# The delta rule's block inverse: VectorE's block transpose for the second orientation of levels 1 to 5

## Chip, cores and metric

The kernel runs on one core of a Trainium2 chip, as one launch. The metric is the device time of the launch in microseconds; the trace gives the span of the core, which is about 2 us shorter.

## What is computed

Two transformer blocks on 256 tokens of width 1024 in fp32: a gated delta rule with a short convolution, sparse attention, MLPs, spatial gating, stick-breaking attention. The change lies in the first mixer, the delta rule. For each of 8 heads and each chunk of 64 tokens the reference solves with a unit lower triangular matrix:

```python
m_low = jnp.where(strict, jnp.einsum('nbhik,nbhjk->nbhij', kb, kc) * decay, 0.0)
a_mat = m_low + jnp.eye(c, dtype=f32)
u = lax.linalg.triangular_solve(a_mat, vc * bc[..., None], left_side=True, lower=True, unit_diagonal=True)
w = lax.linalg.triangular_solve(a_mat, kb * jnp.exp(gc)[..., None], left_side=True, lower=True, unit_diagonal=True)
attn = jnp.einsum('nbhik,nbhjk->nbhij', qc, kc) * decay
...
v_new = u_c - jnp.einsum('bhck,bhkv->bhcv', w_c, state)
o_c = (jnp.einsum('bhck,bhkv->bhcv', q_c * jnp.exp(g_c)[..., None], state)
       + jnp.einsum('bhij,bhjv->bhiv', attn_c, v_new))
```

Here c is 64.

## The kernel before

The weights of all products come as one stream of panels of 1 MB each: SyncE loads a panel into one of four slots of `raw`, ScalarE rounds it to `w_hi`, VectorE writes the rest to `w_lo` (L2238, the "split"), and TensorE multiplies with both. A load into a slot waits until VectorE has split what was there. Every engine has its instructions in an order written out by hand, and semaphores tie them together.

In the delta rule a tile `tt` is 128 tokens, two chunks of 64, one on partitions 0 to 63 and one on 64 to 127; there are two tiles. For one tile the 8 heads ("units") lie side by side, so that `[128, 8, 64]` holds 16 matrices of 64x64. The kernel inverts the 16 triangular matrices of a tile by doubling the block size: level 1 has blocks of 2 rows, level 6 of 64. X is the inverse so far. `gd_zt` is the transposed matrix, `gd_ml` its part that belongs to the level (GpSimd, "POOL", multiplies `gd_zt` with a 0/1 mask, `masks`), and a level computes P = M X and then X - X P. A matmul needs its left factor transposed, so the kernel keeps two orientations: `gd_xx` for X and `gd_xt` for its transpose. From level 1 to level 5 a matrix is block-diagonal with blocks of at most 32.

Per level and tile:
- `level_p` on TensorE: P into PSUM bank 6 + tt (operands `gd_xx` and `gd_ml`, semaphore `gd_pp`), ScalarE copies it to `gd_p` (L2034, `gd_ps`);
- `level_x` on TensorE: `X P` into bank 2 + 2 tt (the x batch, operands `gd_p` and `gd_xt`, `gd_dx`), and in the second orientation into bank 3 + 2 tt (operands `gd_xt` and `gd_p`, `gd_dt_`);
- VectorE subtracts the first from `gd_xx` (L2791, `gd_xi`) and the second from `gd_xt` (L2793, `gd_iv`).

Level 6 has only the second orientation, since the solutions need only `gd_xt`. TensorE's order is: p of tile 0, p of tile 1, then level_x of tile 0, of tile 1. `gd_xi` of the level before lets a p batch start, `gd_iv` of the level before and `gd_ps` let the x batch start. All these products run through `each_unit` (L1095 to L1100), which issues 16 matmuls of 64x64 and signals at the last one:

```python
for u in range(8):
    for c in range(2):
        done = pe.matmul(ps[half(c), bank, u * 64:(u + 1) * 64], lhs[half(c), u, :], rhs(c, u), ...)
done.then_inc(done_sem, 1)
```

Level 1 needs no product: on VectorE, `level1` writes I minus the masked matrix to `gd_xt` (L2695, L2696), and this stands in VectorE's order between a split of panel 5 and the product L2773, behind which come the splits of panels (6, 0) and (6, 1) that TensorE uses before the inverse. To get `gd_xx`, `first_inverse` on TensorE multiplies `gd_xt` with the identity for each tile, and ScalarE copies the result (L2031).

Behind the inverse: `solutions` (TensorE, L1136 and L1146), then the states of the four chunks in turn (L1184, L1190, L1160, L1171, with VectorE's L2812), the output norm, and the output product, with whose splits the weight stream starts again.

Of the kernel before, what the change touches and what calls it, by code (L numbers as in the profile page):

```python
# [23 lines left out]
ALU = mybir.AluOpType  # L24
# [122 lines left out]
def build(nc, dram, layers=LAYERS):  # L147
# [45 lines left out]
    with ExitStack() as ctx:  # L193
# [236 lines left out]
        gd_x1 = sem("gd_x1")  # L430
# [190 lines left out]
        def _(pe):  # L621
# [403 lines left out]
            def delta_rule():  # L1025
# [76 lines left out]
                def first_inverse(tt):  # L1102
                    pe.wait_ge(gd_x1, tt + 1)
                    each_unit(6 + tt, gd_xt[:, tt], lambda c, u: cst("eye64")[half(c), :], gd_pp)

# [9 lines left out]
                def level_x(level, tt):  # L1115
                    n = TT * (level - 2) + tt
                    if level == 2:
                        pe.wait_ge(gd_in, TT * 6)
                        pe.wait_ge(gd_ts, 6)
                    else:  # L1120
                        pe.wait_ge(gd_iv, n - TT + 1)
                    pe.wait_ge(gd_ps, TT + n + 1)
                    if level < 6:
                        each_unit(2 + 2 * tt, gd_xt[:, tt], lambda c, u: gd_p[half(c), tt, u, :], gd_dx)
                    each_unit(3 + 2 * tt, gd_p[:, tt], lambda c, u: gd_xt[half(c), tt, u, :], gd_dt_)
# [135 lines left out]
                first_inverse(0)  # L1261
                first_inverse(1)
# [292 lines left out]
        def _(act):  # L1555
# [380 lines left out]
            def delta_rule():  # L1936
# [92 lines left out]
                for tt in range(TT):  # L2029
                    act.wait_ge(gd_pp, tt + 1)  # L2030
                    act.activation(gd_xx[:, tt].rearrange("p u i -> p (u i)"), ps[:, 6 + tt, :], ACT.Copy).then_inc(gd_ps, 1)  # L2031
                for n in range(10):
                    act.wait_ge(gd_pp, TT + n + 1)
                    act.activation(gd_p[:, n % 2].rearrange("p u i -> p (u i)"), ps[:, 6 + n % 2, :], ACT.Copy).then_inc(gd_ps, 1)  # L2034
                    if n == 1:
                        evacuate(6)
                    if n == 5:
                        act.wait_ge(gd_yb, 1)
                        act.activation(h_hi[:, 0:4, :], gd_sc[:, :, :], ACT.Copy).then_inc(gd_ybh, 1)
# [189 lines left out]
        def _(dve):  # L2229
# [394 lines left out]
            def delta_rule():  # L2624
# [67 lines left out]
                def level1(tt):  # L2692
# [3 lines left out]
                    dve.tensor_tensor(gd_xt[:, tt], eye, gd_xt[:, tt], ALU.subtract).then_inc(gd_x1, 1)  # L2696
# [88 lines left out]
                for level in range(2, 7):  # L2785
                    for tt in range(TT):
# [5 lines left out]
                        dve.wait_ge(gd_dt_, n + 1)  # L2792
# [254 lines left out]
        def _(pool):  # L3047
# [72 lines left out]
            def delta_rule():  # L3120
# [36 lines left out]
                def masks(level):  # L3157
                    for tt in range(TT):
                        if level >= 4:
                            pool.wait_ge(gd_pp, TT * (level - 3) + tt + 1)  # L3160
# [178 lines left out]
```

## Time and profile before

| | us |
|---|---|
| median of 3 runs | 1664.44 (1664.32 to 1664.78) |
| the profiled execution, its own time | 1663.62 |
| span of the profiled execution | 1661.7 |
| TensorE busy in the span | 1634.8 |
| VectorE busy | 1086.3 |
| ScalarE busy | 932.4 |
| GpSimd busy | 89.7 |

The profile is of one execution. Busy times are of instructions only; TensorE's matmuls are pipelined, so a row's time may reach past the start of the next one. An fp32 matmul stands in the trace as two records. A row of the timeline merges like instructions that follow each other (xcount); its second number is then the time from the first start to the last end. `[... <- ...]` at its end is how long the engine was idle before it and what ended that.

### The profile page before, as it was taken

The page shows a single profiled execution, that of the slowest core. Times are in us where ns is not written, and L with a number is a line of the kernel's source. Part 1 is how long each engine was busy: PE and PEld are TensorE (multiplying, and loading weights), DVE is VectorE, ACT ScalarE, POOL GpSimd, SP SyncE. Part 2 cuts the span into 40 slices and gives each one's busy share as a digit, 9 for nine tenths or more (in the row PEclk, how much of TensorE's full clock was granted, in tenths as well). Part 3 has the DMA queues.
Part 4 walks back from the last instruction along what each step waited for, and adds up shares of the span by engine and source line. Part 5 has one row for each costly group of instructions (what it writes and reads, how often), then busy time and mean ns, then how long its engine had stood idle before and what let it go on. Part 6 is the DMA issues. An engine that isn't in the chain of part 4 may idle for free.

```text
span 1661.7 us, 25878 instructions
## 1 busy us (share of the span) xinstructions
PE 1634.8 (98%) x9652; PEld 1375.4 (83%) x9652; DVE 1086.3 (65%) x1552; ACT 932.4 (56%) x1425; POOL 89.7 (5%) x124
## 2 busy tenths in 40 slices
PE   9999999999999999999999999999999999999998
PEld 6898888887668888888888888888888888678886
DVE  5967775555967754677554666775577754777754
ACT  6733664444866644565445546564475645866543
POOL 1431000001000000200001000000010000000000
PEclk9999999999999999999999999999999999999999
DMA  7322455573215554454557444555545555235552
GB/s 277 149 103 89 167 196 187 187 296 132 77 51 178 189 192 183 184 202 178 203 203 264 161 169 167 188 201 202 203 172 182 194 210 181 98 124 201 182 202 102
DMA packets 41346, 291.81 MB, mean 176 GB/s; under 512 B 4880, under 2 KB 5040, under 8 KB 6832
## 3 DMA queue, kind: packets, MB, share of 16 engines
q1 hardware_dynamic: 40000, 282.53, 46.9%
q0 software_dynamic: 1120, 7.88, 1.4%
q8 instruction: 57, 0.93, 0.2%
q10 hardware_dynamic: 144, 0.26, 0.0%
q14 instruction: 25, 0.20, 0.0%
HBM read 289.61 MB, written 1.05 MB: 175 GB/s over the span
## 4 chain that ended last, share of the span: by engine, by line
PE 90%; DVE 3%; ACT 3%; issue 1%; DMA 1%; POOL 1%; SPq 0%; POOLq 0%; ACTq 0%; DVEq 0%
PE ps L676 26%; PE ps L682 13%; PE ps L645 13%; PE ps L653 13%; PE ps L646 13%; PE ps L1098 2%; PE ps L720 1%; DMA raw<-in_stream 1%; DVE w_lo L2238 1%; PE ps L897 1%; PE ps L898 1%; PE ps L906 1%; PE ps L1389 1%; PE ps L1315 0%; ACT w_hi L1571 0%
## 5 line engine op out<-in xcount | busy, mean ns | idle before, releaser
L2238 DVE TENSOR_TENSOR w_lo<-raw,w_hi 128x1024 fp32r<-128x1024 f32 x516 | 612.5, 1215 | 271.8 <-ACT w_hi L1571 271.5
L1571 ACT ACTIVATE w_hi<-raw 128x1024 fp32r<-128x1024 f32 x516 | 518.6, 1039 | 304.6 <-PE ps L653 289.3
L676 PE MATMUL ps<-h_both,w_hi 128*128 128x512 f32 x1920 | 462.9, 392 | 3.3 <-DVE h_both L2252 2.5
L676 PEld LDWEIGHTS ps<-h_both,w_hi 128*128 128x128 f32 x1920 | 352.4, 188 | 73.2 <-DVE h_both L2252 3.7
L645 PE MATMUL ps<-w_hi,hid_hi 128*128 128x512 f32 x660 | 257.8, 391 | 0.2 <-ACT w_hi L1571 0.2
L646 PE MATMUL ps<-w_hi,hid_lo 128*128 128x512 f32 x660 | 256.9, 389 | 0.0
L682 PEld LDWEIGHTS ps<-h_both,w_lo 128*128 128x128 f32 x1920 | 247.9, 191 | 10.4
L682 PE MATMUL ps<-h_both,w_lo 128*128 128x256 f32 x1920 | 251.1, 283 | 0.0
L2320 DVE TENSOR_TENSOR tm<-ps,tm 128x512 f32<-128x512 f32 x120 | 82.9, 691 | 154.3 <-ACT tm L1677 153.9
L653 PE MATMUL ps<-w_lo,hid_hi 128*128 128x512 f32 x660 | 177.6, 389 | 0.0
L1677 ACT ACTIVATE tm<-ps 128x512 f32<-128x512 f32 x120 | 71.7, 598 | 178.8 <-PE ps L682 178.8
L645 PE MATMUL ps<-w_hi,h_both 128*128 128x512 f32 x368 | 147.0, 399 | 2.2 <-ACT w_hi L1571 2.2
L645 PEld LDWEIGHTS ps<-w_hi,hid_hi 128*128 128x128 f32 x660 | 124.0, 188 | 25.9 <-ACT w_hi L1571 0.6
L653 PEld LDWEIGHTS ps<-w_lo,hid_hi 128*128 128x128 f32 x660 | 123.9, 188 | 25.7
L646 PEld LDWEIGHTS ps<-w_hi,hid_lo 128*128 128x128 f32 x660 | 123.9, 188 | 25.2
L646 PE MATMUL ps<-w_hi,h_both 128*128 128x512 f32 x368 | 143.6, 390 | 0.0
L653 PE MATMUL ps<-w_lo,h_both 128*128 128x512 f32 x368 | 98.7, 390 | 0.7 <-DVE w_lo L2238 0.7
L645 PEld LDWEIGHTS ps<-w_hi,h_both 128*128 128x128 f32 x368 | 69.1, 188 | 18.7 <-DVE h_both L2252 3.2
L653 PEld LDWEIGHTS ps<-w_lo,h_both 128*128 128x128 f32 x368 | 69.0, 188 | 15.6 <-DVE w_lo L2238 1.1
L646 PEld LDWEIGHTS ps<-w_hi,h_both 128*128 128x128 f32 x368 | 69.2, 188 | 13.4
L1693 ACT ACTIVATE hid_hi<-inner 128x256 f32 (+3 forms) x120 | 57.0, 475 | 19.8 <-DVE inner L2336 14.6
L1582 ACT ACTIVATE h_both<-ps,norm_t 128x256 fp32r<-128x256 f32 x80 | 31.4, 475 | 59.2 <-PE ps L720 59.2
(354 smaller groups left out, 1388.2 us busy)
## 6 DMA issues: line engine op xcount, KB each, us to landing
raw<-in_stream SPq DMA_DIRECT2D x265, 1024.0 KB, 4.8
ns_w<-in_ns_w POOLq DMA_DIRECT2D x1, 4096.0 KB, 15.7
ln_rows<-in_ln_rows POOLq DMA_DIRECT2D x2, 1024.0 KB, 9.7
const<-in_const SPq DMA_DIRECT2D x1, 1076.0 KB, 11.8
x_sb<-in_x SPq DMA_DIRECT2D x2, 512.0 KB, 5.9
raw<-in_stream SPq DMA_DIRECT2D x2, 512.0 KB, 7.4
out<-x_row SPq DMA_DIRECT2D x3, 256.0 KB, 2.4
row<-in_fin_rows SPq DMA_DIRECT2D x1, 512.0 KB, 18.4
```

Source lines behind the costliest of these rows:

```text
L645: pe.matmul(bank[tt], a_hi[:, k_at + k, rows], hi, start=(k == 0), stop=False)
L646: pe.matmul(bank[tt], a_lo[:, k_at + k, rows], hi, start=False, stop=False)
L653: done = pe.matmul(bank[tt], a_hi[:, k_at + k, rows], lo, start=False, stop=(k == q.kt - 1))
L676: pe.matmul(bank[c], w_hi[:, slot, cols], h_both[:, :, k, :], start=(k == 0), stop=False)
L682: done = pe.matmul(bank[c][:, 0:T], w_lo[:, slot, cols], h_hi[:, k, :], start=False, stop=(k == 7))
L1098: done = pe.matmul(ps[half(c), bank, u * 64:(u + 1) * 64], lhs[half(c), u, :], rhs(c, u), start=(u == 0), stop=True, skip_group_check=True)
L1571: act.activation(w_hi[:, static % 2, part], raw[:, static % RING, part], ACT.Copy).then_inc(hi_ready, 1)
L1582: done = act.activation(h_hi[:, k, :], tps[:, f, :], ACT.Copy, scale=scale)
L1677: act.activation(tm[:, 0, :].rearrange("p (c t) -> p c t", t=T), two[bank][:, :, T:], ACT.Copy).then_inc(low_sums, 1)
L1693: act.activation(hid_hi2[:, bass.ds(b * width, width)], inner[:, bs % 2, 0:width], ACT.Copy).then_inc(t_hi, 1)
L2238: dve.tensor_tensor(w_lo[:, static % 2, part], raw[:, static % RING, part], w_hi[:, static % 2, part].bitcast(F32), ALU.subtract).then_inc ...
L2320: dve.tensor_tensor(by_tile(tm[:, 1, :]), two[bank][:, :, 0:T], by_tile(tm[:, 0, :]), ALU.add).then_inc(hid_sum, 1)
```

## The change

- `first_inverse` is gone from TensorE, and with it ScalarE's two copies. `level1` on VectorE ends with a transpose of `gd_xt` to `gd_xx` and signals `gd_ps` itself.
- In levels 2 to 5 `level_x` no longer multiplies for the second orientation. VectorE waits for its own subtraction (`gd_xi`) and transposes `gd_xx` to `gd_xt`; this signals `gd_iv`.
- VectorE's transpose works on blocks of 32x32: each block of 32 partitions and 32 columns is turned in its place. That is the full transpose as long as the blocks off the diagonal of the 64x64 matrices are zero, which holds up to level 5. Level 6 multiplies as before.
- `gd_pp` counts two batches fewer, so the targets of ScalarE and of GpSimd's masks are two lower, and `gd_dt_` counts level 6 only.

```diff
--- before.py
+++ after.py
@@ -427,7 +427,6 @@
         gd_kk = sem("gd_kk")
         gd_m = sem("gd_m")
         gd_a = sem("gd_a")
-        gd_x1 = sem("gd_x1")
         gd_mlr = sem("gd_mlr")
         gd_pp = sem("gd_pp")
         gd_ps = sem("gd_ps")
@@ -1099,10 +1098,6 @@
                                              start=(u == 0), stop=True, skip_group_check=True)
                     done.then_inc(done_sem, 1)
 
-                def first_inverse(tt):
-                    pe.wait_ge(gd_x1, tt + 1)
-                    each_unit(6 + tt, gd_xt[:, tt], lambda c, u: cst("eye64")[half(c), :], gd_pp)
-
                 def level_p(level, tt):
                     n = TT * (level - 2) + tt
                     pe.wait_ge(gd_mlr, n + 1)
@@ -1122,6 +1117,7 @@
                     pe.wait_ge(gd_ps, TT + n + 1)
                     if level < 6:
                         each_unit(2 + 2 * tt, gd_xt[:, tt], lambda c, u: gd_p[half(c), tt, u, :], gd_dx)
+                        return
                     each_unit(3 + 2 * tt, gd_p[:, tt], lambda c, u: gd_xt[half(c), tt, u, :], gd_dt_)
 
                 def solutions(tt):
@@ -1258,8 +1254,6 @@
                 block_t(5)
                 multiply(q, 6, 6, 0, 1, h_hi, h_lo)
                 pe.wait_ge(gd_tks, 8)
-                first_inverse(0)
-                first_inverse(1)
                 for level in range(2, 7):
                     for tt in range(TT):
                         level_p(level, tt)
@@ -2026,11 +2020,8 @@
                 evacuate(5)
                 split(q, 6, 6, 0, 1)
                 store(5)
-                for tt in range(TT):
-                    act.wait_ge(gd_pp, tt + 1)
-                    act.activation(gd_xx[:, tt].rearrange("p u i -> p (u i)"), ps[:, 6 + tt, :], ACT.Copy).then_inc(gd_ps, 1)
                 for n in range(10):
-                    act.wait_ge(gd_pp, TT + n + 1)
+                    act.wait_ge(gd_pp, n + 1)
                     act.activation(gd_p[:, n % 2].rearrange("p u i -> p (u i)"), ps[:, 6 + n % 2, :], ACT.Copy).then_inc(gd_ps, 1)
                     if n == 1:
                         evacuate(6)
@@ -2693,7 +2684,9 @@
                     mask = cst("level1").unsqueeze(1).broadcast_to([P, 8, 64])
                     eye = cst("eye64").unsqueeze(1).broadcast_to([P, 8, 64])
                     step(dve.tensor_tensor(gd_xt[:, tt], gd_zt[:, tt], mask, ALU.mult))
-                    dve.tensor_tensor(gd_xt[:, tt], eye, gd_xt[:, tt], ALU.subtract).then_inc(gd_x1, 1)
+                    step(dve.tensor_tensor(gd_xt[:, tt], eye, gd_xt[:, tt], ALU.subtract))
+                    dve.transpose(gd_xx[:, tt].rearrange("p u i -> p (u i)"),
+                                  gd_xt[:, tt].rearrange("p u i -> p (u i)")).then_inc(gd_ps, 1)
 
                 def products(tt, bank):
 
@@ -2789,7 +2782,10 @@
                         if level < 6:
                             dve.wait_ge(gd_dx, n + 1)
                             dve.tensor_tensor(x, x, ps[:, 2 + 2 * tt, :], ALU.subtract).then_inc(gd_xi, 1)
-                        dve.wait_ge(gd_dt_, n + 1)
+                            dve.wait_ge(gd_xi, n + 1)
+                            dve.transpose(xt, x).then_inc(gd_iv, 1)
+                            continue
+                        dve.wait_ge(gd_dt_, tt + 1)
                         dve.tensor_tensor(xt, xt, ps[:, 3 + 2 * tt, :], ALU.subtract).then_inc(gd_iv, 1)
                     if level == 2:
                         dve.wait_ge(gd_ts, 6)
@@ -3157,7 +3153,7 @@
                 def masks(level):
                     for tt in range(TT):
                         if level >= 4:
-                            pool.wait_ge(gd_pp, TT * (level - 3) + tt + 1)
+                            pool.wait_ge(gd_pp, TT * (level - 4) + tt + 1)
                         pool.tensor_tensor(gd_ml[:, level % 2, tt], gd_zt[:, tt],
                                            cst(f"level{level}").unsqueeze(1).broadcast_to([P, 8, 64]), ALU.mult).then_inc(gd_mlr, 1)
```

The order of the instructions, at the places where engines wait for each other. The lines of the changed kernel have other numbers: there L1098 is L1097, L2791 is L2784.

TensorE at the start of the inverse, before the change (two rows are one batch of 16; `const,gd_xt` is level 1, `gd_xx,gd_ml` a p batch, `gd_p,gd_xt` an x batch, `gd_xt,gd_p` the second orientation):

```order
L1098 MATMUL ps<-const,gd_xt 64x64 [waits gd_x1,gd_tks]
L1098 MATMUL ps<-const,gd_xt 64x64 x15
L1098 MATMUL ps<-const,gd_xt 64x64 [waits gd_x1]
L1098 MATMUL ps<-const,gd_xt 64x64 x15
L1098 MATMUL ps<-gd_xx,gd_ml 64x64 [waits gd_ps,gd_mlr]
L1098 MATMUL ps<-gd_xx,gd_ml 64x64 x15
L1098 MATMUL ps<-gd_xx,gd_ml 64x64 [waits gd_ps,gd_mlr]
L1098 MATMUL ps<-gd_xx,gd_ml 64x64 x15
L1098 MATMUL ps<-gd_p,gd_xt 64x64 [waits gd_ps,gd_ts,gd_in]
L1098 MATMUL ps<-gd_p,gd_xt 64x64 x15
L1098 MATMUL ps<-gd_xt,gd_p 64x64 x16
L1098 MATMUL ps<-gd_p,gd_xt 64x64 [waits gd_ps,gd_ts,gd_in]
```

The same place after the change:

```order
L1097 MATMUL ps<-gd_xx,gd_ml 64x64 [waits gd_ps,gd_mlr,gd_tks]
L1097 MATMUL ps<-gd_xx,gd_ml 64x64 x15
L1097 MATMUL ps<-gd_xx,gd_ml 64x64 [waits gd_ps,gd_mlr]
L1097 MATMUL ps<-gd_xx,gd_ml 64x64 x15
L1097 MATMUL ps<-gd_p,gd_xt 64x64 [waits gd_ps,gd_ts,gd_in]
L1097 MATMUL ps<-gd_p,gd_xt 64x64 x15
L1097 MATMUL ps<-gd_p,gd_xt 64x64 [waits gd_ps,gd_ts,gd_in]
L1097 MATMUL ps<-gd_p,gd_xt 64x64 x15
```

The two batches of level 1 and the x16 row behind each x batch are gone, and the first p batch now waits on `gd_ps` from VectorE.

VectorE in level 1, before and then after:

```order
L2695 TENSOR_TENSOR gd_xt<-gd_zt,const 128x512 [waits gd_m]
L2696 TENSOR_TENSOR gd_xt<-const,gd_xt 128x512 [waits dve_step]
L2695 TENSOR_TENSOR gd_xt<-gd_zt,const 128x512
L2696 TENSOR_TENSOR gd_xt<-const,gd_xt 128x512 [waits dve_step]
L2773 TENSOR_TENSOR gd_ch<-gd_ch,ps 128x4x256 [waits gd_ts,gd_tp]
L2238 TENSOR_TENSOR w_lo<-raw,w_hi 128x1024 [waits hi_ready] x4
```

```order
L2686 TENSOR_TENSOR gd_xt<-gd_zt,const 128x512 [waits gd_m]
L2687 TENSOR_TENSOR gd_xt<-const,gd_xt 128x512 [waits dve_step]
L2688 STREAM_TRANSPOSE gd_xx<-gd_xt 128x512 [waits dve_step]
L2686 TENSOR_TENSOR gd_xt<-gd_zt,const 128x512
L2687 TENSOR_TENSOR gd_xt<-const,gd_xt 128x512 [waits dve_step]
L2688 STREAM_TRANSPOSE gd_xx<-gd_xt 128x512 [waits dve_step]
L2766 TENSOR_TENSOR gd_ch<-gd_ch,ps 128x4x256 [waits gd_ts,gd_tp]
L2229 TENSOR_TENSOR w_lo<-raw,w_hi 128x1024 [waits hi_ready] x4
```

A STREAM_TRANSPOSE stands behind the subtraction of each tile, each waiting for the instruction ahead; the product L2773 (now L2766) and the four splits come behind them.

VectorE in level 2, before and then after:

```order
L2791 TENSOR_TENSOR gd_xx<-gd_xx,ps 128x512 [waits gd_dx,dve_step]
L2793 TENSOR_TENSOR gd_xt<-gd_xt,ps 128x512 [waits gd_dt_]
L2791 TENSOR_TENSOR gd_xx<-gd_xx,ps 128x512 [waits gd_dx]
L2793 TENSOR_TENSOR gd_xt<-gd_xt,ps 128x512 [waits gd_dt_]
L2796 TENSOR_TENSOR gd_sc<-gd_sc,gd_b 128x1024 [waits gd_ts]
```

```order
L2784 TENSOR_TENSOR gd_xx<-gd_xx,ps 128x512 [waits gd_dx,dve_step]
L2786 STREAM_TRANSPOSE gd_xt<-gd_xx 128x512 [waits gd_xi]
L2784 TENSOR_TENSOR gd_xx<-gd_xx,ps 128x512 [waits gd_dx]
L2786 STREAM_TRANSPOSE gd_xt<-gd_xx 128x512 [waits gd_xi]
L2792 TENSOR_TENSOR gd_sc<-gd_sc,gd_b 128x1024 [waits gd_ts]
```

The second subtraction, which waited for TensorE's `gd_dt_`, is now a transpose that waits for the first one.

## Rows read from the trace of the kernel before

**Rows 1.** The page, parts 1 and 4: busy time; the chain by engine
```profile
PE 1634.8 (98%) x9652; PEld 1375.4 (83%) x9652; DVE 1086.3 (65%) x1552; ACT 932.4 (56%) x1425; POOL 89.7 (5%) x124
...
PE 90%; DVE 3%; ACT 3%; issue 1%; DMA 1%; POOL 1%; SPq 0%; POOLq 0%; ACTq 0%; DVEq 0%
```

**Rows 2.** The chain that ended last, in order of time: start us, us, what
```profile
104.42 28.52 PE ps L1098 x960
```

**Rows 3.** Windows: us, busy PE, PEld, DVE, ACT, POOL, clock, DMA share
```profile
111.97:117.63 5.66, 5.66 (x200) 5.66 (x196) 3.89 (x5) 1.19 (x2) 3.20 (x2) 1.00 0.03 6
...
132.78:146.64 13.86, 11.71 (x358) 11.06 (x354) 8.96 (x16) 5.49 (x7) 0.00 (x0) 1.00 0.02 4
```

**Rows 4.** Instructions of line L1098: duration min/median/max ns, first and last start
```profile
L1098 PE MATMUL ps<-gd_p,gd_xt x256: 218/218/267, 108.2 to 128.0; 64*64 64x64 f32 x128
...
L1098 PE MATMUL ps<-const,gd_xt x64: 218/218/267, 104.4 to 106.2; 64*64 64x64 f32 x64
```

**Rows 5.** Timeline of the inverse: start us, us, engine line op, idle before
```profile
104.35 2.08 PE L1098 MATMUL ps<-const,gd_xt 64*64 64x64 f32 x64
...
111.97 2.06 PE L1098 MATMUL ps<-gd_xx,gd_ml 64*64 64x64 f32 x64
...
113.13 0.60 ACT L2034 ACTIVATE gd_p<-ps 128x512 f32<-128x512 f32 x1 [2.98 <-PE ps L1098]
113.18 3.20 POOL L3161 TENSOR_TENSOR gd_ml<-gd_zt,const 128x512 f32<-128x512 f32 x2 [3.16 <-PE ps L1098]
...
113.88 1.15 PE L1098 MATMUL ps<-gd_p,gd_xt 64*64 64x64 f32 x32
...
115.06 0.69 DVE L2791 TENSOR_TENSOR gd_xx<-gd_xx,ps 128x512 f32<-128x512 f32 x1 [1.04 <-PE ps L1098]
...
121.29 2.05 POOL L3180 TENSOR_TENSOR gd_kz<-gd_k,gd_exp 128x512 f32<-128x512 f32 x2
...
123.72 2.50 POOL L3187 TENSOR_TENSOR gd_z<-gd_z,gd_onorm 128x512 f32<-128x512 f32 x2
...
130.86 2.08 PE L1098 MATMUL ps<-gd_xt,gd_p 64*64 64x64 f32 x64
...
132.04 0.69 DVE L2793 TENSOR_TENSOR gd_xt<-gd_xt,ps 128x512 f32<-128x512 f32 x1 [1.04 <-PE ps L1098]
```

**Rows 6.** Timeline of level 1 and the split behind it, all engines
```profile
86.64 3.34 POOL L3175 TENSOR_TENSOR gd_v<-gd_v,gd_kss 128x512 f32<-128x512 f32 x2 [9.04 <-ACT gd_v L2024]
...
86.95 0.69 DVE L2695 TENSOR_TENSOR gd_xt<-gd_zt,const 128x512 f32<-128x512 f32 x1
...
87.67 1.42 DVE L2696 TENSOR_TENSOR gd_xt<-const,gd_xt 128x512 f32<-128x512 f32 x1
...
89.01 1.53 DVE L2695 TENSOR_TENSOR gd_xt<-gd_zt,const 128x512 f32<-128x512 f32 x1
...
91.18 1.21 DVE L2773 TENSOR_TENSOR gd_ch<-gd_ch,ps 128x1024 f32<-128x1024 f32 x1
...
92.31 2.35 DVE L2238 TENSOR_TENSOR w_lo<-raw,w_hi 128x1024 fp32r<-128x1024 f32 x2
...
94.30 1.07 PE L653 MATMUL ps<-w_lo,h_both 128*128 128x512 f32 x4
```

**Rows 7.** Groups of VectorE by form: xcount | busy us, mean ns
```profile
L2499 DVE TENSOR_TENSOR sgu_z<-sgu_z,ln_rows 128x2048 f32<-128x2048 f32 x2 | 4.6, 2292 | 0.1
...
L2496 DVE TENSOR_SCALAR sgu_z<-sgu_z,v_stat 128x2048 f32<-128x2048 f32 x2 | 2.7, 1340 | 0.0
...
L2765 DVE TENSOR_REDUCE gd_qss<-gd_sq 128x8 f32<-128x512 f32 x2 | 1.3, 678 | 0.0
```

**Rows 8.** Timeline of the states: a VectorE result and its matmul
```profile
139.04 0.69 DVE L2812 TENSOR_TENSOR gd_vt<-ps,gd_kss 64x512 f32<-64x512 f32 x1 [0.32 <-PE ps L1160]
...
139.78 0.25 PEld L1184 LDWEIGHTS ps<-gd_vt,gd_kz 64*64 64x64 f32 x5 [0.47 <-DVE gd_vt L2812]
```

**Rows 9.** Waits of SyncE's DMA queue: us in total, times, longest
```profile
SPq L589 <- DVE w_lo L2238: 1345.2, 254, 52.4
```

## The prediction

> **What bounds the kernel now.** I read the page first: TensorE is busy for 98% of the span and has 90% of the chain that ended last [rows 1]. A microsecond is worth something only where it leaves TensorE's line. The chain in order of time then shows the place of the change: from 104.42 us on it lies 28.52 us long on L1098 alone, 960 records without a break [rows 2]. That is the block inverse. The windows, cut at the starts of the levels, say why: in a level of 5.66 us TensorE is busy for 5.66, VectorE for 3.89, ScalarE for 1.19, and the weight stream stands still (DMA share 0.03) [rows 3]. The other two engines wait for TensorE here, and nothing else can be the bound before the change.
>
> One call of `each_unit`, "a batch" below, is 16 matmuls, 32 records: 960 records are 30 batches. Six of them make a level of 5.66 us, and the four from the x batch at 113.88 to the level's end at 117.63 take 3.75 [rows 3, 5]. I take 0.935 us for one.
>
> **What the change removes.** The second orientation in levels 2 to 5 is 256 records, 8 batches; turning level 1 is 64 records, 2 batches [rows 4]. Together 10 of the 30 batches, 10 x 0.935 = 9.35 us. That would be the gain if TensorE stayed the bound, but it does not.
>
> **What it adds, and the new chain of a level.** VectorE now subtracts and transposes for tile 0, then the same for tile 1, and TensorE can't start tile 1's next p batch before tile 1's subtraction. The new period comes from the reaction times of the old one [rows 5, 8]:
> - p batch to ScalarE's copy: 113.13 - 111.97 = 1.16 us; the copy 0.60.
> - x batch to the subtraction: 115.06 - 113.88 = 1.18 us; the subtraction 0.69.
> - end of a VectorE result to the matmul that wants it: gd_vt starts at 139.04 and lasts 0.69, the weights load at 139.78, so 0.05. A subtraction's start is then 0.69 + 0.05, say 0.75, ahead of its matmul.
> - VectorE, an instruction that waits for the one ahead: 87.67 - 86.95 = 0.72 from start to start. One that doesn't: L2773 lasts 1.21 and the split starts 1.13 later, so 0.08 is hidden [rows 6].
>
> The transpose itself has no row. The nearest is L2765, which also reads 512 fp32 elements a partition from one SBUF source: 678 ns [rows 7]. The lower bound is a one-source fp32 instruction at two elements a cycle, as L2496 runs (2048 elements in 1340 ns, against 2292 for the two-source L2499) [rows 7]. 512 elements in 0.69 and 2048 in 2.292 leave a fixed part of 0.15 us, so the fast form would take (1.340 - 0.15) / 4 + 0.15 = 0.45 us. The upper bound is four times the lane time, 4 x 0.535 + 0.15 = 2.29 us, as long as L2499. I take 0.69, by L2765.
>
> Let S be the start of tile 0's subtraction. Its transpose starts at S + 0.72; tile 1's subtraction at S + 0.72 + 0.61 = S + 1.33, its x batch being long over; tile 1's p batch at S + 1.33 + 0.75 = S + 2.08. The x batch of tile 0 stands behind it in TensorE's queue and starts at S + 2.08 + 0.935 = S + 3.02; its two operands are earlier (copy done at S + 2.51, transpose at S + 1.41). The next S is 1.18 later, S + 4.20. So **a level takes 4.20 us in place of 5.66**, by a loop through both engines; TensorE works 4 x 0.935 = 3.74 of it. VectorE is through at S + 2.66, and L2796 of level 2, as long as L2773's 1.21, ends at S + 3.9, still covered. The copy of tile 1 ends at S + 3.84 and its x batch starts at S + 3.95: covered by 0.1.
>
> **The sum.** Level 2's p batch starts at 104.35, where the first batch of level 1 does now, since its operand was transposed long before. Then x0 at 104.35 + 1.87 = 106.22 and S = 107.40; three periods on, S of level 5 is 120.00; level 6 has its first batch of `ps<-gd_xt,gd_p` at 120.00 + 3.02 = 123.02, now 130.86 [rows 5]. That is 7.84 us. What follows is as before.
>
> Against it stand the two transposes in level 1, where VectorE has no idle time: level 1 begins at 86.95, the product L2773 at 91.18, and the split that begins at 92.31 (its first half ends 1.22 later, at 93.53) is wanted by TensorE at 94.30 [rows 6]. L2696 of tile 0 and L2695 of tile 1 took 1.42 and 1.53 us in place of 0.69 while POOL's L3175 ran. With the transpose of tile 0 at 89.12, L2695 of tile 1 comes when POOL is nearly done (86.64 + 3.34 = 89.98), so part of the new time falls into what was lost to POOL. L2773 then starts at 89.98 + 0.72 + 0.72 + 0.61 = 92.03, 0.85 late; the half split ends at 94.38, and TensorE is held for 0.15. The halves after it have over a microsecond in hand.
>
> Sum: 7.84 - 0.15 = **7.7 us off**. The profiled execution took 1663.62 us, 0.8 below the median of 1664.44, with a span of 1661.7; the difference should be the same in each. Median: 1664.44 - 7.7 = **1656.8** (1656.75). The rest of the kernel keeps it: SP's loads wait on VectorE's splits [rows 9], so the weight stream moves with the stage. POOL's masks wait for the p batches of two levels before (their target is two lower, as two batches are gone); even at 3.20 us for a pair [rows 5] they end over 3 us before they are wanted. If that cover went, a late mask would cost up to its 1.6 us. gd_kz and gd_z, behind them in POOL's queue, are wanted only after the solutions. ScalarE loses two copies of 0.60 that stood between level 1's batches and level 2's.
>
> **A rule against a row.** The row shows that a VectorE instruction that waits for the one ahead starts 0.72 us after it, against 0.61 for one that doesn't [rows 6]. The Trainium skill, "VectorE: DVE Perf Modes", section "The DRAIN you can't avoid", says that the next operation can't issue until the pipe is empty and that "the semaphore costs nothing extra here". By that rule the wait between subtraction and transpose would be free, three of them in the periods, and the sum would be 3 x 0.11 = 0.3 us larger. The trace speaks against it, so I keep 0.72.
>
> The Trainium skill, "VectorE: DVE Perf Modes", section "The three transpose paths", has 311 ns for a 128x128 bf16 block on VectorE; 384 elements more at 0.96 GHz make an estimate of 711 ns, by which the sum would be 0.1 smaller. No trace of before shows it.
>
> **Rivals.**
> - *Half rate:* two cycles an element, 1.21 us, as 1024 elements take. Four transposes lie on the chain (three periods and the way to level 6): 4 x 0.52 = 2.1 us. L2773 comes 1.65 late and TensorE is held 0.95. 7.84 - 2.1 - 0.95 = 4.8 off: 1659.6. No row speaks for fp32 being halved, none shows a transpose. 0.12.
> - *Double rate,* 0.45 us: 4 x 0.24 and the 0.15 in level 1, 1.1 more: 1655.6. For it L2496, against it L2765 [rows 7]. 0.06.
> - *POOL holds the transposes* as it held L2696 and L2695. It did not lengthen the subtraction at 115.06, with one source in PSUM, though a mask ran then [rows 5]. The transpose has one source too, but in SBUF. Held, level 1 costs 0.6 more, and by the queue of POOL (2.05 for gd_kz, 2.50 for gd_z) [rows 5] the transposes of tile 0 in levels 4 and 5 meet one instruction of these, 0.6 and 0.25. 7.7 - 1.45 = 6.2 off: 1658.2. 0.10.
> - *Three cycles an element,* 1.75 us: 6 transposes bear on the end, 4 on the chain and 2 in level 1, 6 x 1.06 = 6.4, so 1.3 off: 1663.1, no change. 0.04.
> - *Slower, VectorE becomes the bound.* At 2.29 us a level is 2 x (0.72 + 2.21) = 5.86 on VectorE, and L2796 and L2799 (1.13 each) no longer have a gap. S of level 5 is 107.40 + 1.13 + 3 x 5.86 = 126.11; two subtractions with transposes and L2799 later, the subtraction of level 6 starts at 133.10, now at 132.04 [rows 5]: 1.1 later. In level 1 L2773 comes 3.8 late and TensorE is held 3.1. Sum 4.2 slower: 1668.6. The change turns into a loss at 0.69 + 7.7 / 6 = 1.97 us a transpose. For it: nothing shows how fp32 passes the block. Against: no fp32 row here shows less than an element a cycle. 0.04.
> - *The clock.* TensorE gets pauses of 0.06 and 0.40 us in a level. Right behind the stage it is busy 11.71 of 13.86 us, 84%, at a granted clock of 1.00 [rows 3]; the new level has 89%. If the clock fell to 1.2 GHz, the 11 batches on the chain would take 0.935 longer each, 10.3: 1664.44 - 7.7 + 10.3 = 1667.1. The Trainium skill, "TensorE: Matmul & The Clock Gate", Part 1, has the clock follow how busy the array has been of late; by that rule pauses can lower it, which the trace so far does not bear out. 0.02.
>
> **How the numbers follow.** The forecast has 0.62. A measurement of this kernel can tell 0.2%, 3.3 us, from no change: 1661.1 to 1667.8. Faster: 0.62 + 0.12 + 0.06 + 0.10 = 0.90; same: 0.04 + 0.02 = 0.06; slower: 0.04. The range reaches from the double rate to the half rate, with 0.2 and 0.4 us beyond: 1655.4 to 1660.0.
>
> **What would show it.** L1098 with 640 matmul records in place of 960. A transpose of about 0.69 us. Starts of `ps<-gd_xx,gd_ml` 4.2 us apart. TensorE waiting for gd_xx before tile 1's p batch, VectorE for TensorE before tile 0's subtraction. L653 near 94.3 held for 0.2 us or not at all. The chain passing through VectorE's gd_xx and gd_xt. I am wrong in the mechanism if the period is far from 4.2, and wrong in the carry if the stage ends 7 us earlier and the kernel does not.

## The result, and the profile after

| us | before | after |
|---|---|---|
| median on the same chip | 1664.38 (1663.92 to 1664.96, 6 runs) | 1656.39 (1656.16 to 1656.97, 6 runs) |
| the profiled execution | 1663.62 | 1656.41 |
| its span | 1661.7 | 1654.6 |
| predicted | | 1656.8 (1655.4 to 1660.0) |

The changed kernel is faster: the medians differ by 7.99 us; the ratio of the runs is 0.9946, with a 95% interval of 0.9935 to 0.9957, which is 9.0 us off, 7.2 to 10.8. The two profiled executions differ by 7.2 us, their spans by 7.1. Of the twelve executions behind the table's medians, any one of after lies 6.95 to 8.80 us below any one of before, so the 9.0 of the ratio is more than any pair of them shows. On the chip of the first four experiments, five of the 23 executions of before took 1668.7 to 1670.0 us, at a mean granted clock of 0.994 where the others have 0.998 to 1.000, and so the ratios there show larger gains than the medians.

The page after, parts 1 and 4 (it answers to [rows 1]):

```profile
PE 1627.6 (98%) x9332; PEld 1366.8 (83%) x9332; DVE 1086.9 (66%) x1554; ACT 931.1 (56%) x1423; POOL 90.0 (5%) x124
...
PE 90%; DVE 4%; ACT 3%; issue 1%; DMA 1%; POOL 1%; SPq 0%; POOLq 0%; ACTq 0%; DVEq 0%
```

TensorE has 320 records and 7.2 us of work less. Over the whole span VectorE's share of the chain went from 3% to 4%; inside the block inverse much more changed. The chain from 104 to 126 us, where before it was one piece of 28.52 us on one line [rows 2], first by line and then one turn of it in order of time (start us, us, what):

```profile
by line: PE ps L1097 46.8%; DVE gd_xx L2784 22.9%; DVE gd_xt L2786 16.2%; DVE gd_sc L2792 7.6%; PE ps L652 3.1%; issue 2.9%; PE ps L1132 1.3%; DVEq L2783 0.1%
...
116.22 0.70 DVE gd_xx L2784
116.92 0.02 issue
116.94 0.71 DVE gd_xt L2786
117.66 0.59 DVE gd_xx L2784
118.24 0.14 issue
118.38 2.10 PE ps L1097 x64
120.47 0.02 issue
120.50 0.70 DVE gd_xx L2784
```

This is the loop through both engines: VectorE subtracts and transposes for tile 0 and subtracts for tile 1, TensorE makes tile 1's p batch and tile 0's x batch, and then VectorE subtracts again.

The windows of levels 3 and 4, cut like [rows 3] at the starts of tile 0's p batches (which makes the level of [rows 3] level 3), then 13.86 us across the levels (us, busy PE, PEld, DVE, ACT, POOL, clock, DMA share, GB/s):

```profile
108.45:112.79 4.34, 4.17 (x129) 4.01 (x129) 4.27 (x6) 1.19 (x2) 3.06 (x2) 1.00 0.01 4
112.79:117.06 4.27, 4.10 (x131) 3.99 (x129) 2.68 (x5) 2.14 (x3) 3.38 (x4) 1.00 0.02 4
...
104.43:118.29 13.86, 13.43 (x417) 12.92 (x416) 8.95 (x13) 5.73 (x10) 10.18 (x8) 1.00 0.01 4
```

A level is down from 5.66 to 4.27 us, TensorE has 0.17 us of pause in it, and its clock stays at 1.00. In the first window, into which the product L2792 falls, VectorE has work for 4.27 of 4.34 us: one level in which it is nearly the bound.

Line L1097, once L1098 [rows 4] (duration min/median/max ns, first and last start), and the transpose:

```profile
L1097 PE MATMUL ps<-gd_xx,gd_ml x320: 218/218/267, 104.4 to 123.6; 64*64 64x64 f32 x160
...
L1097 PE MATMUL ps<-gd_p,gd_xt x256: 218/218/267, 106.4 to 121.2; 64*64 64x64 f32 x128
...
L1097 PE MATMUL ps<-gd_xt,gd_p x64: 218/218/267, 123.6 to 125.5; 64*64 64x64 f32 x64
```

```profile
L2786 DVE STREAM_TRANSPOSE gd_xt<-gd_xx x8: 711/711/712, 108.3 to 122.5; 128x512 f32<-128x512 f32 x8
```

640 records are left of 960. The transpose takes 0.711 us, to the nanosecond the same in all eight, though GpSimd worked beside several of them.

The timeline of the inverse (as [rows 5]):

```profile
107.62 0.69 DVE L2784 TENSOR_TENSOR gd_xx<-gd_xx,ps 128x512 f32<-128x512 f32 x1 [5.60 <-PE ps L1097]
108.34 0.71 DVE L2786 STREAM_TRANSPOSE gd_xt<-gd_xx 128x512 f32<-128x512 f32 x1
...
108.98 0.65 DVE L2784 TENSOR_TENSOR gd_xx<-gd_xx,ps 128x512 f32<-128x512 f32 x1
...
109.69 3.49 POOL L3157 TENSOR_TENSOR gd_ml<-gd_zt,const 128x512 f32<-128x512 f32 x2 [1.51 <-PE ps L1097]
...
109.77 1.15 PE L1097 MATMUL ps<-gd_xx,gd_ml 64*64 64x64 f32 x32 [0.17 <-DVE gd_xx L2784]
110.30 1.75 DVE L2792 TENSOR_TENSOR gd_sc<-gd_sc,gd_b 128x1024 f32<-128x1024 f32 x1
...
111.97 0.67 DVE L2784 TENSOR_TENSOR gd_xx<-gd_xx,ps 128x512 f32<-128x512 f32 x1
...
119.33 2.12 PE L1097 MATMUL ps<-gd_p,gd_xt 64*64 64x64 f32 x64
...
120.50 0.69 DVE L2784 TENSOR_TENSOR gd_xx<-gd_xx,ps 128x512 f32<-128x512 f32 x1 [1.52 <-PE ps L1097]
...
123.60 2.12 PE L1097 MATMUL ps<-gd_xt,gd_p 64*64 64x64 f32 x64
```

Level 6 starts at 123.60 where it started at 130.86: 7.26 earlier. The output product behind the states starts at 139.46, before at 146.67, 7.21 earlier, and the span ends 7.1 earlier. The gain is made in one stage and carried whole.

Level 1 (as [rows 6]):

```profile
86.55 3.34 POOL L3171 TENSOR_TENSOR gd_v<-gd_v,gd_kss 128x512 f32<-128x512 f32 x2 [9.05 <-ACT gd_v L2018]
86.84 0.69 DVE L2686 TENSOR_TENSOR gd_xt<-gd_zt,const 128x512 f32<-128x512 f32 x1
87.56 1.42 DVE L2687 TENSOR_TENSOR gd_xt<-const,gd_xt 128x512 f32<-128x512 f32 x1
...
89.02 0.71 DVE L2688 STREAM_TRANSPOSE gd_xx<-gd_xt 128x512 f32<-128x512 f32 x1
89.65 0.78 DVE L2686 TENSOR_TENSOR gd_xt<-gd_zt,const 128x512 f32<-128x512 f32 x1
...
91.83 1.18 DVE L2766 TENSOR_TENSOR gd_ch<-gd_ch,ps 128x1024 f32<-128x1024 f32 x1
...
94.20 1.21 PE L652 MATMUL ps<-w_lo,h_both 128*128 128x512 f32 x4
```

The product L2766 starts at 91.83, before at 91.18 [rows 6], and TensorE's L652 takes 1.21 in place of 1.07: it is held for 0.14. From the start of L652 to the start of the inverse it is 10.23 us, before 10.05, so the inverse starts 0.18 later for it.

### The profile page after: what moved, and what is told of

The parts are those of the page before. It is cut to its first block, busy times and chain, and to the rows that moved or that the text cites. A ratio compares the mean times of both kernels' runs of the same rounds, so it can differ in the third digit from the quotient of the medians.

```text
span 1654.6 us, 25237 instructions
## 1 busy us (share of the span) xinstructions
PE 1627.6 (98%) x9332; PEld 1366.8 (83%) x9332; DVE 1086.9 (66%) x1554; ACT 931.1 (56%) x1423; POOL 90.0 (5%) x124
## 4 chain that ended last, share of the span: by engine, by line
PE 90%; DVE 4%; ACT 3%; issue 1%; DMA 1%; POOL 1%; SPq 0%; POOLq 0%; ACTq 0%; DVEq 0%
PE ps L675 26%; PE ps L681 14%; PE ps L644 13%; PE ps L652 13%; PE ps L645 13%; PE ps L719 1%; DMA raw<-in_stream 1%; DVE w_lo L2229 1%; PE ps L896 1%; PE ps L1097 1%; PE ps L897 1%; PE ps L905 1%; PE ps L1383 1%; PE ps L1309 0%; ACT w_hi L1565 0%
## 5 line engine op out<-in xcount | busy, mean ns | idle before, releaser
L652 PE MATMUL ps<-w_lo,hid_hi 128*128 128x512 f32 x660 | 177.6, 389 | 0.0
L652 PEld LDWEIGHTS ps<-w_lo,hid_hi 128*128 128x128 f32 x660 | 123.9, 188 | 25.7
L652 PE MATMUL ps<-w_lo,h_both 128*128 128x512 f32 x368 | 98.9, 390 | 0.7 <-DVE w_lo L2229 0.7
L652 PEld LDWEIGHTS ps<-w_lo,h_both 128*128 128x128 f32 x368 | 68.9, 188 | 15.9 <-DVE w_lo L2229 1.4
```

The costliest lines, as they stand in the source:

```text
L652: done = pe.matmul(bank[tt], a_hi[:, k_at + k, rows], lo, start=False, stop=(k == q.kt - 1))
```

## The experiments

All diffs are against the changed kernel, and leave out what only renames or counts semaphores. "The stage" is the time from TensorE's first batch of the inverse to the start of level 6's last product (`ps<-gd_xt,gd_p`), and a level's window goes from the start of its p batch to that of the next level. A median stands with its range and its number of runs; each ratio is against the kernel before on the same chip. For the first four kernels below that had a median of 1665.11 us, for the one with three transposes and the one with the product moved ahead 1664.29, for the others 1663.88.

**One part of the change alone: level 1.** Levels 2 to 5 multiply for both orientations again.

```diff
-                        return
...
-                            dve.wait_ge(gd_xi, n + 1)
-                            dve.transpose(xt, x).then_inc(gd_iv, 1)
-                            continue
-                        dve.wait_ge(gd_dt_, tt + 1)
+                        dve.wait_ge(gd_dt_, n + 1)
```

> Only the level 1 part of the change: VectorE transposes gd_xt once per tile, levels 2 to 5 multiply for both orientations as before. Theory A (what is removed from TensorE's line is gained until a loop through VectorE and TensorE binds): the first p batch starts 1.93 us earlier (106.29 to about 104.4), against it the hold of 0.15 us of L653 near 94.2, so 1.8 us off: 1662.6 us, levels still 5.66 us. Rival B (the two transposes in VectorE's full stretch cost what they save): 1664.2 or more, with a hold of over 1 us before the inverse.

Measured: 1662.77 us (1661.23 to 1663.66, 12 runs), ratio 0.9978 (0.9969 to 0.9987). Two batches of 0.97 us are gone from TensorE, and L652 took 1.21 as in the changed kernel, so 1.94 - 0.14 = 1.8 us should be gained; the medians give 2.3. Levels 2 to 5 take 5.69, 5.66, 5.92 and 5.68 us. Level 4 has a batch that took 1.35 us in place of 1.13, at full clock, and no wait that the trace names; the others are as before.

**The other part alone: levels 2 to 5.**

```diff
+                def first_inverse(tt):
+                    pe.wait_ge(gd_x1, tt + 1)
+                    each_unit(6 + tt, gd_xt[:, tt], lambda c, u: cst("eye64")[half(c), :], gd_pp)
...
+                first_inverse(0)
+                first_inverse(1)
...
+                for tt in range(TT):
+                    act.wait_ge(gd_pp, tt + 1)
+                    act.activation(gd_xx[:, tt].rearrange("p u i -> p (u i)"), ps[:, 6 + tt, :], ACT.Copy).then_inc(gd_ps, 1)
...
-                    step(dve.tensor_tensor(gd_xt[:, tt], eye, gd_xt[:, tt], ALU.subtract))
-                    dve.transpose(gd_xx[:, tt].rearrange("p u i -> p (u i)"),
-                                  gd_xt[:, tt].rearrange("p u i -> p (u i)")).then_inc(gd_ps, 1)
+                    dve.tensor_tensor(gd_xt[:, tt], eye, gd_xt[:, tt], ALU.subtract).then_inc(gd_x1, 1)
```

> Only the levels 2 to 5 part: TensorE multiplies with the identity for level 1 as before, VectorE transposes in levels 2 to 5. Theory A: the rest of the gain, 7.26 - 1.8 = 5.5 us off: 1658.9 us, level periods 4.27 to 4.34 us, no hold near 94.2. If the two parts helped or hindered each other, e1 and e2 would not add up to the whole change (7.2 to 8.0 us off).

Measured: 1659.39 (1658.61 to 1660.40, 6 runs), ratio 0.9958 (0.9943 to 0.9974), 5.7 us by the medians. From the first p batch (106.34) to level 6 (125.49) it is 19.15 us, in the changed kernel 19.17 and before 24.57, and there is no hold in L652. By the traces the parts add up: 24.57 - 19.15 = 5.4 and 1.8 make the 7.2 of the two profiled executions. By the medians they are 5.7 and 2.3, the 8.0 of the whole. The ratios give 7.0 and 3.7 against 9.0, each with an interval of over a microsecond to either side, so they can't test the sum that finely.

**The removed work put back.** TensorE issues the eight batches of levels 2 to 5 again, on other operands and for no one's use; VectorE goes on transposing.

```diff
                         each_unit(2 + 2 * tt, gd_xt[:, tt], lambda c, u: gd_p[half(c), tt, u, :], gd_dx)
+                        each_unit(3 + 2 * tt, gd_p[:, tt], lambda c, u: cst("eye64")[half(c), :], gd_dt_)
                         return
```

> The change with 8 batches of TensorE put back in levels 2 to 5, of the size of the removed ones (gd_p against the identity, results not used), so that TensorE's line is as long as before while VectorE still transposes. Theory A (the gain is TensorE's time): a level is 5.66 us again and only level 1's gain is left, 1.8 us off: 1662.6 us. Rival C (the gain comes from the shorter wait of VectorE, which has its operand at hand instead of waiting for TensorE's second product): most of the gain stays, 1658 us or less.

Measured: 1662.28 (1661.54 to 1664.28, 12 runs), ratio 0.9979 (0.9970 to 0.9988). The window of its level 4:

```profile
116.28:121.94 5.66, 5.66 (x200) 5.66 (x197) 2.80 (x4) 2.14 (x3) 4.45 (x4) 1.00 0.01 3
```

The period is back at the 5.66 of before, without a pause on TensorE; levels 2 to 5 take 5.75, 5.67, 5.66 and 5.70. The rival C of the expectation, 1658 us or less, is out. The gain of the levels is TensorE's removed work; VectorE's two chains of transposes and subtractions cost nothing where TensorE has the batches to cover them.

**The order on VectorE.** Both subtractions ahead of both transposes, so that tile 1's p batch needn't wait for tile 0's transpose.

```diff
+                    for tt in range(TT if level < 6 else 0):
+                        n = TT * (level - 2) + tt
+                        x = gd_xx[:, tt].rearrange("p u i -> p (u i)")
+                        dve.wait_ge(gd_dx, n + 1)
+                        dve.tensor_tensor(x, x, ps[:, 2 + 2 * tt, :], ALU.subtract).then_inc(gd_xi, 1)
                     for tt in range(TT):
...
-                            dve.wait_ge(gd_dx, n + 1)
-                            dve.tensor_tensor(x, x, ps[:, 2 + 2 * tt, :], ALU.subtract).then_inc(gd_xi, 1)
```

> The change with VectorE's order in a level turned to: subtract tile 0, subtract tile 1, transpose tile 0, transpose tile 1. Theory A says the period is set by tile 0's transpose standing ahead of tile 1's subtraction: tile 1's subtraction starts at S + 0.94 to 1.0 (when its x batch is done) in place of S + 1.36, so its p batch follows tile 0's without a pause and a level takes 3.8 to 3.9 us in place of 4.27, close to the four batches of TensorE (3.74). 4 x 0.4 = 1.6 us faster than the changed kernel: 1654.8 us. Rival D (VectorE's amount of work in a level, with its waits, sets the period, not its order): same as the changed kernel, 1656.4 us.

Measured: 1655.75 (1655.56 to 1656.51, 6 runs), ratio 0.9936 (0.9921 to 0.9951). Its windows by level:

```profile
108.65:112.98 4.33, 4.01 (x128) 3.89 (x129) 4.30 (x6) 1.20 (x2) 3.10 (x2) 1.00 0.02 4
112.98:116.93 3.95, 3.94 (x128) 3.90 (x129) 2.36 (x4) 2.14 (x3) 3.10 (x4) 1.00 0.01 4
```

The second window, level 4, takes 3.95 us with TensorE busy for 3.94 of it: it is the bound again, and the 0.32 us a level that were left in the loop are gone. Level 3 keeps 4.33, since L2795 (L2792 in the changed kernel) took 1.73 us beside GpSimd's mask and made the next subtraction late. From the first p batch to level 6 it is 18.18 us, 0.99 less than in the changed kernel, and not 1.6 as expected. The median lies between the 1654.8 of theory A and the 1656.4 of rival D, and the changed kernel did not run on this chip; what decides for theory A is the windows, in which VectorE has the same instructions in another order and a level is shorter.

**The changed kernel once more,** on one chip with three others: the copy, the doubled transpose, and the last kernel of this section.

> The changed kernel itself, on the chip on which the next ones run, so that they can be compared with it and not only with the kernel before. 7.2 to 8.0 us below the kernel before, as in the first comparison.

Measured: 1656.62 (1656.31 to 1657.50, 5 runs), ratio 0.9951 (0.9937 to 0.9964), 7.3 us below before by the medians. Its profile has the inverse from 105.54 to 124.71, 19.17 us as in the first profile, but all of it 1.11 us later, and its span is 1.1 us longer (1655.7). The two executions part early in the span:

```profile
10.00:15.00 5.00, 4.61 (x14) 3.57 (x15) 2.45 (x2) 1.31 (x2) 3.59 (x8) 0.66 1.03 430
```

The same five microseconds in the first profile of the same kernel:

```profile
10.00:15.00 5.00, 5.00 (x28) 4.20 (x27) 2.52 (x4) 2.59 (x6) 3.31 (x8) 1.00 1.02 421
```

One execution has a mean granted clock of 0.66 there and another 1.00, with the first weights still arriving. Of the twelve profiles of this study two have the 0.66, this one and that of the kernel with level 1 alone, and they start the inverse last, at 105.54 and 105.74 us. The other ten have 1.00 there and start it between 103.23 and 104.86, so the clock does not explain all of the spread; what makes the rest is open.

**A copy in the transpose's place.** The kernel leaves out the turning, so its result is not the inverse; only its time is of use. It tells what a shorter instruction would give, and what GpSimd does to it.

```diff
-                            dve.transpose(xt, x).then_inc(gd_iv, 1)
+                            dve.tensor_copy(xt, x).then_inc(gd_iv, 1)
```

> The changed kernel with a plain copy of gd_xx to gd_xt in place of the transpose in levels 2 to 5 (the turning is left out). It shows the price of a faster one-source instruction and whether POOL holds such a one. By the fast form of L2496 a copy takes 0.45 us. Theory A: 4 x 0.26 = 1.0 us less than the changed kernel, 1655.4 us, if it isn't held. Rival (POOL holds one-source instructions that read SBUF fast): copies of over 0.8 us where POOL's L3157 or L3176 runs, and most of the 1.0 us gone.

Measured: 1656.71 (1655.93 to 1657.13, 5 runs), ratio 0.9952 (0.9938 to 0.9965): nothing gained. Its timeline:

```profile
108.75 0.43 DVE L2786 COPY gd_xt<-gd_xx 128x512 f32<-128x512 f32 x1
109.04 3.48 POOL L3157 TENSOR_TENSOR gd_ml<-gd_zt,const 128x512 f32<-128x512 f32 x2 [1.51 <-PE ps L1097]
109.10 2.29 DVE L2792 TENSOR_TENSOR gd_sc<-gd_sc,gd_b 128x1024 f32<-128x1024 f32 x1
...
113.37 2.69 POOL L3157 TENSOR_TENSOR gd_ml<-gd_zt,const 128x512 f32<-128x512 f32 x2 [0.84 <-PE ps L1097]
113.43 1.49 DVE L2786 COPY gd_xt<-gd_xx 128x512 f32<-128x512 f32 x1
```

Alone the copy takes 0.43 us; beside GpSimd's instructions it took 0.78, 1.49, 0.96, 0.55 and 0.53, and the stage is 19.38 us long, 0.21 more than with the transpose. The rival of the expectation holds, and its theory A does not. The rival "POOL holds the transposes" describes this fast copy, and not the transpose with its constant 0.711.

**The transpose twice.**

```diff
                             dve.wait_ge(gd_xi, n + 1)
+                            step(dve.transpose(xt, x))
                             dve.transpose(xt, x).then_inc(gd_iv, 1)
```

> The changed kernel with each transpose of levels 2 to 5 done twice, the second waiting for the first (0.74 us more each, 16 transposes in place of 8). Theory A: one of the two transposes of a level lies on the loop, so a level takes 4.27 + 0.74 = 5.0 us, and four of them make 3.0 us: 3.0 us above the changed kernel, 1659.4 us. If both lay on the chain, 6 us; if neither, nothing.

Measured: 1660.07 (1658.47 to 1661.58, 7 runs), ratio 0.9972 (0.9961 to 0.9984), 3.45 us above the changed kernel on the same chip. The window of its level 3:

```profile
108.81:114.08 5.27, 4.23 (x129) 4.01 (x129) 5.13 (x8) 1.20 (x2) 3.24 (x2) 1.00 0.01 3
```

The stage is 22.34 us long, 3.17 more. Four transposes lie on the chain (three periods and the way to level 6), as the prediction counted, so one costs 3.17 / 4 = 0.79. By parts it is 0.74 to 0.75 in three of the four, which is what lies from start to start of one of the doubled transposes to the next, and 0.93 in level 3, where VectorE, with the product of `gd_sc` with `gd_b` as well, is busy for 5.13 of the 5.27 us.

**And three times,** the same edit with one line more.

> The changed kernel with each transpose of levels 2 to 5 done three times, 2.2 us in a row, the price at which the rival of the prediction had VectorE as the bound. A level has 2 x (0.72 + 2 x 0.75 + 0.61) = 5.7 us of VectorE, and the loop through TensorE takes 4.27 + 1.5 = 5.8. Theory A: periods of 5.8, in level 2 and 5 up to 1 us more for the two products that have no gap left, so 4 x 1.5 + 1 to 2 = 7 to 8 us above the changed kernel: 1663.5 to 1664.6 us, the kernel before's time, though TensorE does 10 batches less. If the slope of one transpose on the loop (3.0 to 3.4 us for four, e8) went on in a line, 6.0 to 6.9 us above it.

Measured: 1664.81 (1663.86 to 1665.52, 11 runs), ratio 1.0001 (0.9992 to 1.0010): the whole gain is gone at some 2.2 us for three transposes in a row, level 1's being left single. The expectation ended at 1664.6. Four windows of it, the first one a level and the next ones from the level behind:

```profile
108.04:115.18 7.14, 4.38 (x129) 4.03 (x129) 6.93 (x10) 1.20 (x2) 2.54 (x2) 1.00 0.01 2
115.20:117.99 2.79, 1.13 (x32) 1.02 (x33) 2.69 (x5) 0.60 (x1) 1.27 (x1) 0.89 0.00 0
117.99:119.20 1.21, 1.21 (x23) 1.21 (x25) 1.18 (x2) 0.00 (x0) 0.00 (x0) 0.50 0.05 14
119.20:120.70 1.50, 1.50 (x34) 1.50 (x33) 0.85 (x2) 0.70 (x2) 0.66 (x1) 0.50 0.00 0
```

The first window is level 3, and VectorE is busy for 6.93 of its 7.14 us; in level 5 it is 5.70 of 5.94. VectorE is the bound or next to it, as the rival for "slower" had it. With it came a second loss: in the third of TensorE's waits, of 1.66, 1.03 and 1.66 us, the granted clock fell to 0.50, 1.2 GHz, for some 3 us, and a p batch that takes 1.15 us took 1.97. That level, level 4, took 7.01 us, the next one, at full clock, 5.94. So about 1.1 us of the loss is the clock, by this comparison of two levels, and without it the stage, 27.71 us long, would be about as long as the 26.51 of before. Two later waits, of 1.66 and 1.53 us, went by without a fall.

**The product L2792 moved ahead of the levels,** VectorE's order otherwise as in the changed kernel.

```diff
+                dve.wait_ge(gd_ts, 6)
+                dve.tensor_tensor(gd_sc[:, :, :], gd_sc[:, :, :], gd_b[:, :, :], ALU.mult).then_inc(gd_yb, 1)
                 for level in range(2, 7):
...
-                    if level == 2:
-                        dve.wait_ge(gd_ts, 6)
-                        dve.tensor_tensor(gd_sc[:, :, :], gd_sc[:, :, :], gd_b[:, :, :], ALU.mult).then_inc(gd_yb, 1)
```

> The changed kernel in its own order, with only the product of gd_sc with gd_b moved ahead of the levels. In the changed kernel it ends at about the time at which level 3's subtraction may start (111.97 by the trace, 110.73 + 1.18 = 111.91 by its x batch), so Theory A says: under 0.1 us gained, 1656.4 us; the product matters only in the grouped order, where the period is shorter. Rival: POOL's mask and the product, which hold each other up, cost the stage more than the trace shows, and 0.5 us or more goes.

Measured: 1656.16 (1655.25 to 1656.34, 5 runs), ratio 0.9948 (0.9934 to 0.9962). The stage is 19.04 us, 0.13 shorter. Level 3 now takes 4.27 us as well, against 4.34: that much the product had cost there. The rest lies ahead of level 3, whose p batch comes 3.95 us behind level 2's in place of 4.02. The rival, 0.5 us or more, is out.

**The best of it:** both subtractions first, the product ahead of the levels, and level 1's transposes behind the splits of panel 6. The first two edits are those shown above; the third is this:

```diff
-                    dve.transpose(gd_xx[:, tt].rearrange("p u i -> p (u i)"),
-                                  gd_xt[:, tt].rearrange("p u i -> p (u i)")).then_inc(gd_ps, 1)
...
+                for tt in range(TT):
+                    dve.transpose(gd_xx[:, tt].rearrange("p u i -> p (u i)"),
+                                  gd_xt[:, tt].rearrange("p u i -> p (u i)")).then_inc(gd_x1, 1)
```

> The grouped order of e4, and two more edits: level 1's transposes stand behind the splits of panel 6, and the product of gd_sc with gd_b (in e4 1.73 us long while POOL's mask ran, and in the way of level 3's subtraction, period 4.33 against 3.95) stands ahead of the levels, where VectorE waits over 5 us. Theory A: the hold of 0.13 us at L653 goes, the period of 4.33 becomes 3.95: 0.5 us less than e4, 1.6 us less than the changed kernel: about 1654.8 us. Rival: POOL's masks then hold something else of VectorE, and it stays within 0.2 us of e4.

Measured: 1655.01 (1654.33 to 1655.92, 5 runs), ratio 0.9942 (0.9929 to 0.9956). It is 1.6 us below the changed kernel on the same chip and the lowest median here. The trace shows 1.2 of it: the stage is 18.11 us, 1.06 shorter, and L653 (L652 in the changed kernel) is no longer held (1.07 us), which is worth 0.18. Levels 2 and 3 take 3.95 us, but levels 4 and 5 take 4.17 and 4.09: the p batches there took 2.37 and over 2.23 us in place of 2.08, without another engine's work that the trace names as the cause. So the stage is only 0.07 shorter than in the grouped order, where 0.4 was expected. The cause of the long batches is open; one stands in level 4 of the kernel with level 1 alone too, so this order of VectorE is not needed for it.

## Why the prediction was right in its mechanism, and where its sum failed

- **The step that failed** is "the difference should be the same in each": the sum took what one profiled execution gains in the stage as the difference of the medians, and put the difference between executions outside the stage at nothing. The runs show in its place 7.1 us between the spans of the profiled executions, 8.0 between the medians and 9.0 (7.2 to 10.8) by the ratio, against 7.7 forecast. The profiled execution of before was 0.8 us below its median, that of after at its median. The low edge of the range, 1655.4, had no term for this, and the ratio lands on that edge: 1664.44 x 0.9946 = 1655.5, with an interval that reaches 1.8 us to either side. The second profile of the changed kernel shows such a difference, 1.1 us from start to end with a stage of the same 19.17. Which of 7.3, 8.0 and 9.0 is the gain of the change alone is not settled: the traces account for 7.2, the second comparison has 7.3 by the medians and 8.2 by the ratio, and where the rest comes from is open.
- **The sum of the stage** failed too, the other way. Predicted 7.84 from the start of the inverse to level 6; measured 26.51 - 19.17 = 7.34. The missing 0.50 are the first subtraction, 3.19 us behind the first batch in place of 3.05 (0.14), three periods of 4.35, 4.25 and 4.28 in place of 4.20 (0.28), and 3.10 in place of 3.02 to level 6 (0.08). That the median came within 0.4 us of the forecast is luck: a stage that gained 0.5 too little and 0.8 from outside it set each other off.
- **The bound before, and what goes.** Right. 640 records are left of 960, and with the eight batches put back the period is 5.66 again.
- **The price of the transpose.** 0.711 us against 0.69 taken from L2765. The rivals that gave it another rate, from double to a quarter, fall with it, and so does the one that had GpSimd hold it. The estimate by the Trainium skill, "VectorE: DVE Perf Modes", section "The three transpose paths", was 711 ns: the trace agrees to the nanosecond.
- **The loop of a level.** The form is right, the length 0.08 short: 0.72 + 0.64 + 0.80 + 0.95 + 1.17 = 4.28 us from 116.22 to 120.50, against 0.72 + 0.61 + 0.75 + 0.935 + 1.18 = 4.20. From the subtraction to its matmul it was 0.80, since the shorter times of [rows 8] were taken from another place, and the start of tile 1's subtraction behind a transpose came 0.03 later than assumed.
- **L2796 is "still covered".** Nearly: it took 1.75 us and not 1.21, since GpSimd's mask fell on it, and it ended when the next subtraction was due. The run with the product moved ahead puts this at 0.07 in the period.
- **Level 1.** Counted from its first instruction (86.95 and 86.84), the product was 0.76 us late, not 0.85: tile 1's first instruction did not wait for the end of GpSimd's, as assumed, but started at 89.65 and took 0.78, so the transpose of tile 0 filled the time that had been lost to GpSimd. The hold is 0.14 in L652 and 0.18 up to the inverse, predicted 0.15.
- **The carry.** Right: 7.26 us at level 6, 7.21 at the output product, 7.1 at the end. The 7.26 are 7.34 of the stage less an inverse that starts 0.08 later. No mask is waited for.
- **The rule against the row.** The period kept 0.72 us for an instruction that waits for the one ahead, and 0.64 behind the transpose for one that doesn't. So the row was the right one to go by. The Trainium skill's "the semaphore costs nothing extra here" ("VectorE: DVE Perf Modes", "The DRAIN you can't avoid") is said of eight copies, and the prediction stretched it to this pair; the same section says that an instruction which isn't held starts earlier, and with that the trace agrees.
- **The clock.** It stayed at 1.00 with pauses of 0.17 us. The prediction's 89% for a level was counted by batches of 0.935 us and compared with 84% of the profile's busy time; by the profile's count the 13.86 us across the levels are 97% busy, so the comparison was of two different measures. The kernel with three transposes shows the rival's mechanism at work, with pauses above a microsecond.

## What to carry to other kernels

Where an engine at its bound makes something that another can make as well, the gain is the removed work minus the loop that takes its place: add up the reaction times once around (here 4.28 us against the 3.95 of a level in which TensorE is the bound), and order the helper's instructions so that the result the bound engine waits for comes first. That reordering, both subtractions ahead of both transposes, gave another 1.0 us of the stage for no work. Give a range a term for how the executions of one kernel differ outside the stage.

## What was not expected of the hardware

- A plain fp32 copy from SBUF to SBUF is faster than the transpose alone (0.43 against 0.71 us) and not in company: up to 1.49 us while GpSimd ran, where the transpose never left 0.711. The Trainium skill, "GPSIMD Engine Reference", section "1. Specifications", has GpSimd contend with VectorE's instructions in a two-port mode or with two SBUF inputs; the held copy, and L2792 with two SBUF inputs (1.23 us alone in the kernel with the product moved ahead, 1.75 and 2.29 under the masks), agree, and the transpose would then be neither. The loss can also fall on GpSimd: in the kernel with two transposes the product took 1.18 us beside a mask, and the mask 2.35 in place of 1.27.
- With pauses of 1.66, 1.03 and 1.66 us between its batches TensorE's granted clock fell from 1.00 to 0.50 in the middle of the inverse, for about 3 us, and did not fall with 1.66 and 1.53 us later in the same execution; in the other kernels here it stayed at 1.00 there, in the one with two transposes too, with pauses of 0.92 us.
- At the very start executions of the same kernel differ: 0.66 or 1.00 of the clock between 10 and 15 us, and the execution with 0.66 starts the inverse 1.1 us later and ends 1.1 us later.
